# Attention moved one block forward against the gate units in a two-block kernel on one core

## The reference, cut to what matters

```python
def diff_attend(q, k, v, lam):
    s = jnp.einsum('bqhid,bkhid->bhiqk', q, k) * ATTN_SCALE
    p = jax.nn.softmax(s, axis=-1)
    a = p[:, :, 0] - lam * p[:, :, 1]
    return jnp.einsum('bhqk,bkhe->bqhe', a, v)
...
    y = jax.nn.sigmoid(ga) * (attn @ w_ao) + jax.nn.sigmoid(gf) * (four @ w_fo)
    return y @ w_o
```

## Time and profile before

| | us |
|---|---|
| runs | 994.3, 992.0, 992.61; median 992.61 |
| the profiled execution | 992.18 |
| its span | 990.3 |
| TensorE busy | 945.9 |
| VectorE busy | 620.3 |
| ScalarE busy | 421.3 |
| GpSimd busy | 87.7 |

### The profile page before, as it was taken

One profiled execution on the slowest core, in us unless ns is written; L12 is line 12 of the kernel. 1 busy time (PEld: TensorE's weight loads), 2 busy tenths in 40 slices (PEclk: granted clock), 3 DMA queues, 4 the chain that ended last, 5 costly groups with the idle time before them and its releaser, 6 DMA issues.

```text
span 990.3 us, 13527 instructions
## 1 busy us (share of the span) xinstructions
PE 945.9 (96%) x5361; PEld 712.5 (72%) x5361; DVE 620.3 (63%) x849; ACT 421.3 (43%) x612; POOL 87.7 (9%) x73
## 2 busy tenths in 40 slices
PE   3999999998999999999999999999999999999996
PEld 3998777878999999998898766667786334343432
DVE  4567778687667777767877847876656242333334
ACT  4545962664454334435634345565324122221112
POOL 5001000000000000000000044544100000000000
PEclk9999999999999999999999999999997999999998
DMA  9745787634667778766595572224794899999992
GB/s 330 251 160 177 255 327 295 225 128 140 233 226 285 264 261 304 265 205 207 168 364 179 174 255 85 85 86 162 269 381 196 344 420 420 422 418 421 419 421 113
DMA packets 79873, 255.99 MB, mean 259 GB/s; under 512 B 4503, under 2 KB 8350, under 8 KB 66366
## 3 DMA queue, kind: packets, MB, share of 16 engines
q1 hardware_dynamic: 77200, 248.59, 67.6%
q0 software_dynamic: 1632, 5.04, 1.6%
q10 hardware_dynamic: 974, 1.45, 0.5%
HBM read 254.01 MB, written 1.05 MB: 258 GB/s over the span
## 4 chain that ended last, share of the span: by engine, by line
PE 82%; DVE 9%; DMA 3%; ACT 3%; issue 3%; POOL 0%; ACTq 0%; POOLq 0%; SPq 0%; DVEq 0%
PE gemm_ps L1276 11%; PE gemm_ps L831 7%; PE gemm_ps L827 7%; PE gemm_ps L833 7%; PE gemm_ps L832 7%; PE gemm_ps L829 7%; PE gemm_ps L828 7%; PE gemm_ps L1322 6%; PE mix_ps L827 2%; PE mix_ps L829 2%; PE mix_ps L828 2%; DMA ring<-in_w_attn_out_dram 1%; DVE w_lo L486 1%; PE mix_ps L1332 1%; PE gemm_ps L1259 1%
## 5 line engine op out<-in xcount | busy, mean ns | idle before, releaser
L480 ACT ACTIVATE w_hi<-ring 128x1024 fp32r<-128x1024 f32 (+2 forms) x222 | 227.0, 1035 | 227.6 <-PE gemm_ps L833 87.4
L486 DVE TENSOR_TENSOR w_lo<-ring,w_hi 128x1024 fp32r<-128x1024 f32 (+2 forms) x202 | 236.3, 1190 | 112.1 <-ACT w_hi L480 110.9
L831 PE MATMUL gemm_ps<-acts,w_hi 128*128 128x256 f32 x640 | 184.7, 289 | 5.7 <-DVE acts L1904 3.3
L833 PE MATMUL gemm_ps<-acts,w_lo 128*128 128x256 f32 x640 | 181.6, 284 | 0.0
L832 PE MATMUL gemm_ps<-acts,w_hi 128*128 128x256 f32 x640 | 181.6, 284 | 0.0
L827 PE MATMUL gemm_ps<-w_hi,acts 128*128 128x512 f32 (+2 forms) x448 | 177.2, 396 | 3.8 <-DVE w_lo L486 2.9
L829 PE MATMUL gemm_ps<-w_hi,acts 128*128 128x512 f32 (+2 forms) x448 | 170.2, 380 | 0.0
L828 PE MATMUL gemm_ps<-w_lo,acts 128*128 128x512 f32 (+2 forms) x448 | 170.0, 379 | 0.0
L831 PEld LDWEIGHTS gemm_ps<-acts,w_hi 128*128 128x128 f32 x640 | 123.4, 193 | 8.3 <-issue 3.6
L832 PEld LDWEIGHTS gemm_ps<-acts,w_hi 128*128 128x128 f32 x640 | 123.4, 193 | 1.8 <-issue 1.4
L833 PEld LDWEIGHTS gemm_ps<-acts,w_lo 128*128 128x128 f32 x640 | 123.3, 193 | 0.0
(11 more groups left out here) (366 smaller groups left out, 1289.3 us busy)
## 6 DMA issues: line engine op xcount, KB each, us to landing
ring<-in_w_in_dram SPq DMA_DIRECT2D x56, 1024.0 KB, 5.6
ring<-in_w_mod_dram SPq DMA_DIRECT2D x32, 1024.0 KB, 5.3
ring<-in_w_ffn_in_dram SPq DMA_DIRECT2D x20, 1024.0 KB, 7.1
late_ring<-in_w_exp_down_dram SPq DMA_DIRECT2D x20, 1024.0 KB, 15.0
late_ring<-in_w_exp_gate_dram SPq DMA_DIRECT2D x18, 1024.0 KB, 14.1
late_ring<-in_w_exp_up_dram SPq DMA_DIRECT2D x18, 1024.0 KB, 12.3
ring<-in_w_ffn_out_dram SPq DMA_DIRECT2D x11, 1024.0 KB, 5.7
ring<-in_w_exp_up_dram SPq DMA_DIRECT2D x9, 1024.0 KB, 14.2
```

Source lines behind the costliest of these rows:

```text
L480: nc.scalar.activation(part(w_hi, u), raw_unit(u), ACT.Copy).then_inc(hi_made, 1)
L486: eng.tensor_tensor(part(w_lo, u), raw_unit(u), part(w_hi, u), ALU.subtract).then_inc(lo_made[unit["maker"]], 1)
L831: mm(dst, wh, xh, start=a_, stop=False, skip_group_check=True)
L833: last = mm(dst, wl, xh, start=False, stop=b_, skip_group_check=True)
```

## The change

TensorE computes scores 0 inside the last value product, after its third unit. In the loop, behind gate unit n, now stand scores n+1, turn n and heads out n-1. The wait for `kv_ready` moves to just ahead of heads out 0, the wait for `four_B` ahead of the first `fo` unit. ScalarE computes exponentials 0 ahead of the copies of the last value product. VectorE, GpSimd and SyncE have the same code as before.

```diff
+            def first_scores():
+                pe.wait_ge(sem("rope_done"), 8)
+                scores(0)
...
-                product(index["v"][c], rows(step["v"] + c, lambda t: tokens(0, t)), after_unit=ropes(6) + fourier(2) if c == 0 else fourier(3))
-            pe.wait_ge(sem("rope_done"), 8)
+                product(index["v"][c], rows(step["v"] + c, lambda t: tokens(0, t)), after_unit=ropes(6) + fourier(2) if c == 0 else fourier(3) + [first_scores])
...
-            pe.wait_ge(sem("four_B"), 4)
-            pe.wait_ge(sem("kv_ready"), 8)
             N = HEADS2 * TT
-            for n in range(N + 2):
-                if n < N:
-                    c, q = n // 4, n % 4
-                    p = step["g2"] + c
-                    if q == 0:
-                        pair_free_wait(pe, p)
-                    product_unit(units_of[index["g2"][c]][q], rows(p, lambda t: tokens(0, t)), True, True)
-                    scores(n)
-                elif n == N:
+            for n in range(N):
+                c, q = n // 4, n % 4
+                p = step["g2"] + c
+                if q == 0:
+                    pair_free_wait(pe, p)
+                product_unit(units_of[index["g2"][c]][q], rows(p, lambda t: tokens(0, t)), True, True)
+                if n + 1 < N:
+                    scores(n + 1)
+                else:
+                    pe.wait_ge(sem("four_B"), 4)
                     pair_free_wait(pe, y0)
                     pair_free_wait(pe, y0 + 1)
                     fo_unit(0)
-                if 1 <= n <= N:
-                    probs_turn(n - 1)
-                if n >= 2:
-                    heads_out(n - 2)
-                if n == N:
-                    fo_unit(1)
+                probs_turn(n)
+                if n == 1:
+                    pe.wait_ge(sem("kv_ready"), 8)
+                if n >= 1:
+                    heads_out(n - 1)
+            fo_unit(1)
+            heads_out(N - 1)
...
+            def exponentials(n):
+                act.wait_ge(sem("nmax"), n + 1)
+                if n >= 2:
+                    act.wait_ge(sem("diff_turned"), n - 1)
+                for c in range(2):
+                    A(PP[:, n % 2, c, :], PM[:, c, :], ACT.Exp, scale=HD ** -0.5, bias=ds[:, 16 + 2 * (n % 2) + c:17 + 2 * (n % 2) + c],
+                      accum_out=ds[:, 20 + 2 * (n % 2) + c:21 + 2 * (n % 2) + c]).then_inc(sem("probs"), 1)
+
+            exponentials(0)
             take_v("v", 1, 2)
...
-                act.wait_ge(sem("nmax"), n + 1)
-                if n >= 2:
-                    act.wait_ge(sem("diff_turned"), n - 1)
-                for c in range(2):
-                    A(PP[:, n % 2, c, :], PM[:, c, :], ACT.Exp, scale=HD ** -0.5, bias=ds[:, 16 + 2 * (n % 2) + c:17 + 2 * (n % 2) + c],
-                      accum_out=ds[:, 20 + 2 * (n % 2) + c:21 + 2 * (n % 2) + c]).then_inc(sem("probs"), 1)
+                if n >= 1:
+                    exponentials(n)
```

More of the change, by code:

```diff
@@ L1077, in fourier_channels, with scores @@
                 mm(PM[:, 3, 0:SEQ], tab("dft_nsin"), DT[:, g % 2, SEQ:512], start=False, stop=True).then_inc(sem("four_2"), 1)
+            def scores(n):
+                hd, t = n // TT, n % TT
+                if n >= 1:
+                    pe.wait_ge(sem("probs"), 2 * n)
+                for c in range(2):
+                    last = mm(PM[:, c, :], QT[c * HD:(c + 1) * HD, hd, t * P:(t + 1) * P], KTT[c * HD:(c + 1) * HD, hd, :], start=True, stop=True)
+                last.then_inc(sem("scores"), 1)
+            def first_scores():
+                pe.wait_ge(sem("rope_done"), 8)
+                scores(0)
             def ropes(j):
@@ L1091, in _ @@
                 pair_free_wait(pe, step["v"] + c)
-                product(index["v"][c], rows(step["v"] + c, lambda t: tokens(0, t)), after_unit=ropes(6) + fourier(2) if c == 0 else fourier(3))
-            pe.wait_ge(sem("rope_done"), 8)
[L1096 to L1099, removed]
-                for c in range(2):
-                    last = mm(PM[:, c, :], QT[c * HD:(c + 1) * HD, hd, t * P:(t + 1) * P], KTT[c * HD:(c + 1) * HD, hd, :], start=True, stop=True)
-                last.then_inc(sem("scores"), 1)
+                product(index["v"][c], rows(step["v"] + c, lambda t: tokens(0, t)), after_unit=ropes(6) + fourier(2) if c == 0 else fourier(3) + [first_scores])
             def probs_turn(n):
```

## The result

| | before | after |
|---|---|---|
| median of the runs, us | 993.45 (992.0 to 994.3, 4 runs) | 1000.66 (999.4 to 1001.1, 4 runs) |
| the profiled execution, its span | 992.18, 990.3 | 1001.14, 999.3 |
| last Fourier product of tokens (L1069) | 572.82 | 575.65 |
| first turn of the heads (L1167 / L1169) | 680.34 | 688.21 |
| between these two | 107.52 | 112.56 |

The change makes the kernel slower: ratio 1.0061, 95% interval 1.0036 to 1.0086. It was timed a second time beside the kernel before, with more runs: 998.93 against 993.7 us, ratio 1.0044 (1.0023 to 1.0065). The forecast was 994.2, and the range ended at 996.5; both medians lie outside.

What follows compares the result with a forecast made beforehand. TensorE, 82% of the span, was taken as the bound, beside a 5.30 us lock loop of nearly equal length. The heads' turn at 682.0 against 680.34 gave +1.6: 992.18 to 993.8, plus 0.43 for the median, 994.2; range 991.3 to 996.5.

Steps and rivals of the forecast that it cites:

- Scores 0: Ahead of the first gate unit: scores 0 start inside the last value product at 581.0, exponentials 0 at 584.75.
- Exponentials 1: In block 1 on ScalarE: held until unit 3's low part on GpSimd ends at 590.5, they start at 590.6.
- The start: Front of the stretch: the 0.9 us of issue goes, gate unit 2 starts at 595.4; 1.6 of 1.8 us won.
- I add 0.4, because L2287 meets the next low part: Block 1, exponentials to turn: 0.4 us on top of 3.01, for a VectorE instruction held by GpSimd's low part.
- The steady loop: Blocks 2 to 14: the high part waits for the unit beside it; period 5.62 against 5.30, gate blocks 6.09 against 5.85.
- The end: Behind unit 15: exponentials 15 wait for gate 3's copies, 3.6 us after the unit's start, then 8.1 to the heads' turn.
- C: Rival, slower: two low parts in line on GpSimd delay block 1's L2279 to 592.9; +3.5 us, 996.1; chance 0.22.
- B: Rival, start's gain kept: the VectorE and GpSimd lock loop keeps the period at 5.30; -1.6 us, 991.0; chance 0.12.
- D: Rival, half the loss: the head's copies are in time, only the diff path counts; period 5.52, 992.9 us; chance 0.18.
- Everything behind shifts as one: Behind the turn of the heads at 682.0: all hangs on TensorE's progress, loads too, and shifts as a whole by +1.6 us.
- Not much more can be won by a better start: Front of the stretch: TensorE's waits there sum to 1.8 us, about the most a better start could win.

Runs made afterwards that it cites:

- the swapped kernel: The changed kernel, with ScalarE doing exponentials of block 1 ahead of the high part of gate unit 4: 996.13 us, ratio 1.0013, stretch 108.82.
- The negated maximum: The swapped kernel, with the tiny 128x2 negated maximum made by ScalarE instead of VectorE: 994.44 us, ratio 0.9999, stretch 107.99.

## Why the prediction was wrong

By its own steps, all times of after less 2.83, which it comes late to L1069:

1. *Scores 0.* Forecast 581.0, measured 581.03 (583.86). Exponentials 0: forecast 584.75, measured 584.80. Right.
2. *Exponentials 1.* Forecast 590.6, measured 590.98. Right to 0.4. The 0.4 is that of the high parts, which start at 587.40 (590.23) instead of 587.0: L2287 ended as soon as unit 3's low part was over (593.78, with the two parts' 4.72 us begun at 591.37), and did not have to wait for unit 4's.
3. *The start.* The 0.9 of "issue" went, as forecast. Gate unit 2: forecast 595.4, measured 598.91, **3.5 us later. This is the step that failed**, and in it the path from exponentials 1 to the turn of block 1, put at 3.01 us and "I add 0.4, because L2287 meets the next low part". That L2287 is the number in the kernel before, where it is the scaling by lambda, L2295 in the changed kernel. Its term was right: the scaling took 0.34 more than bare. What had no term is the next instruction behind it, the difference (now L2296), which is exposed to the ports too. With two high parts back to back on ScalarE and a third right behind the exponentials, GpSimd had work from 591.37 to 598.67 with a gap of 0.24, and the difference, late by the scaling's 0.34, came 0.08 too late for that gap. It took 2.80 instead of 0.75. In place of 0.4 the rows show 0.34 and 2.05, together 2.4. The other part is a thing that the prediction had no step for: TensorE, idle for 2.8 us, did the turn and the heads out partly at the lower clock, 1.2 us more. With the collision out of the way, unit 2 starts at 595.17 in the swapped kernel, 22.53 behind L1069, where the forecast had 22.58.
4. *The steady loop.* Forecast 5.62 and 6.09 for gate blocks, measured 5.60 and 6.02; from unit 2 to unit 15 forecast 74.9, measured 74.79 (601.74 to 676.53). Right, and for the reason given: the high part waits for the unit, and the squares behind it hold the heads. The negated maximum, which took the ports out of the loop, left it at 5.60.
5. *The end.* From unit 15 to the turn of the heads forecast 11.7, measured 11.68. Right, with the idle 0.84 at `fo` unit 0:

```profile
676.53 0.48 PE L827 MATMUL gemm_ps<-w_hi,acts 128*128 128x512 f32 x1
...
679.56 0.60 ACT L1451 ACTIVATE arena<-gemm_ps 128x512 f32<-128x512 f32 x1 [0.76 <-PE gemm_ps L829]
...
680.37 0.47 PE L827 MATMUL gemm_ps<-w_hi,acts 128*128 128x512 f32 x1 [0.84 <-issue]
...
688.21 1.04 PE L1169 MATMUL mix_ps<-tables_sb,arena 128*128 128x128 f32 x8
```

The sum for the stretch was +1.6; the swapped kernel, which is the change without the collision, has +1.3, and the change itself +5.0.

**The rivals.** C had the right cause, GpSimd's low parts in line, and part of the size (+3.5 of 5.0), at the wrong instruction. It put the price, 2.4 us, on the tiny instruction (L2279, now L2287), and weighed whether a second low part wins against an instruction that waits already. Here it didn't: L2287 got through between the two. The loss came at the difference, which arrived when the third had just begun. B and D were wrong about this loop: 5.60 is neither 5.30 nor 5.52, and D came to light only when the squares were moved.

**"Everything behind shifts as one"** held about: 310.0 and 309.2 from the heads' turn to the end for the kernel before, 311.1 and 309.5 for the changed one.

**"Not much more can be won by a better start"** than 1.8 us was said of the start and stands, but as a view of the kernel it missed the larger sum: 4.1 us came off by moving one 128x2 instruction.

**What stays open.** Whether 2.8 us of idle time always bring the lower clock: all three traces that had such an idle stretch here (2.8, 2.8 and 3.0 us) show it, in one from 0.4 us before TensorE resumed, in two from 0.6 us after, and none of the nine others does here. But the length of the idle time was not varied by itself, and elsewhere the same idle time has both outcomes: near 16 us every execution has one of 2.5 to 3.3 us, and of the four with 2.53 or 2.54 us two show the lower clock behind it and two don't. Nor is it known why the lower clock at 119 to 125 us comes in four executions of twelve; the four are among the five in which TensorE resumes there last (at 119.77 to 120.34 us).

## What to carry to other kernels

When a step is moved on one engine, follow not only what it waits for but what it now lets start behind it on a third engine: here two high parts on ScalarE became a closed queue on GpSimd, and a 0.75 us instruction of VectorE that fell into it took 2.80. Ask of every two-input VectorE instruction on the path which GpSimd instruction starts just ahead of it, and price the case in which it comes second at the full length of that one. Ask it of each instruction in a chain: here the scaling's delay of 0.34 us is what put the difference behind the third low part. Before an order is changed, look for tiny instructions that meet a long one on shared ports in every block, and try them on an engine that has its own: that won 4 us where the change of order lost 5.

## What the runs showed of the hardware

- A two-input VectorE difference that comes second waits out GpSimd's whole instruction and ends 0.54 us behind it (599.21 against 598.67, 592.77 against 592.23; 0.55 in the changed kernel's second trace), while a 128x2 instruction of one input ends 0.03 behind it (and 593.78 against 593.75 in the changed kernel).
- Between two low parts that stand in line without a gap, a waiting 128x2 instruction gets in (593.04 to 593.78, within 591.37 to 596.09), and the pair still took only 4.72 us, twice 2.36.
- Three traces of three with TensorE idle for 2.8 to 3.0 us in this stretch show a granted clock below full where it resumes (0.62 in the window from 600 to 603 us in the changed kernel, where it added 1.2 us).
